# MLP and GLU up products: one 512-column matmul for high weights against both operand parts, and the two sums added by ScalarE and VectorE

## The reference, cut to what matters

```python
def _sq_relu_mlp(x, w1, w2):                 # w1: 1024 x 4096, w2: 4096 x 1024, twice
    return jnp.square(jax.nn.relu(x @ w1)) @ w2

def swiglu(h, w_gate, w_up, w_down):         # 1024 x 2816 twice, 2816 x 1024; twice
    return (jax.nn.silu(h @ w_gate) * (h @ w_up)) @ w_down
```

## Time and profile before

| what | value |
|---|---|
| median of 3 runs | 1182.96 us (1181.51 to 1185.43) |
| profiled execution, first to last instruction (span) | 1181.9 us |
| PE busy | 1162.1 us, 98% of the span |
| PEld, DVE, ACT, POOL busy | 1041.8, 658.0, 514.1, 51.0 us |
| share of PE in the chain that ended last | 92% |
| mean DMA rate | 169 GB/s |
| mean granted TensorE clock | 0.993 of full |

### The profile page before, as it was taken

One profiled execution on the slowest core, in us unless ns is written; L12 is line 12 of the kernel. 1 busy time (PEld: TensorE's weight loads), 2 busy tenths in 40 slices (PEclk: granted clock), 3 DMA queues, 4 the chain that ended last, 5 costly groups with the idle time before them and its releaser, 6 DMA issues.

```text
span 1181.9 us, 18506 instructions
## 1 busy us (share of the span) xinstructions
PE 1162.1 (98%) x7660; PEld 1041.8 (88%) x7668; DVE 658.0 (56%) x717; ACT 514.1 (43%) x581; POOL 51.0 (4%) x93
## 2 busy tenths in 40 slices
PE   9999999999999999999999999999999999999997
PEld 7997999998977799999889999989988878999996
DVE  4757554555654755545654544467854565544543
ACT  4433444443544344444344443445635644434342
POOL 1000000000200100000000000010120010000000
PEclk9999999999999999999999999998989999999999
DMA  9664656554641565565346555556651144456541
GB/s 338 220 211 146 213 178 197 182 180 120 211 161 36 177 219 179 190 183 187 127 144 213 178 177 177 198 156 202 192 164 37 37 161 139 149 181 206 189 148 54
DMA packets 140908, 199.67 MB, mean 169 GB/s; under 512 B 9240, under 2 KB 119024, under 8 KB 140864
## 3 DMA queue, kind: packets, MB, share of 16 engines
q1 hardware_dynamic: 138160, 190.27, 50.0%
q0 software_dynamic: 2704, 8.79, 2.4%
HBM read 197.99 MB, written 1.05 MB: 168 GB/s over the span
## 4 chain that ended last, share of the span: by engine, by line
PE 92%; DVE 3%; ACT 2%; DMA 2%; POOL 1%; issue 1%; SPq 0%; DVEq 0%; POOLq 0%; ACTq 0%
PE up L1401 15%; PE up L1403 15%; PE up L1402 15%; PE acc L1434 11%; PE acc L1435 11%; PE acc L1437 11%; DMA raw<-in_sc_w_in 2%; PE acc L1507 1%; PE up L1489 1%; PE up L1850 1%; PE up L1876 1%; PE up L1478 1%; PE up L1873 1%; PE up L1743 1%; PE up L1423 1%; PE up L1427 1%
## 5 line engine op out<-in xcount | busy, mean ns | idle before, releaser
L933 DVE TENSOR_TENSOR weight_lo<-raw,weight_hi 128x2048 fp32r<-128x2048 f32 (+3 forms) x206 | 414.4, 2017 | 312.4 <-ACT weight_hi L569 312.2
L1401 PE MATMUL up<-xh,weight_hi 128*128 128x256 f32 x1548 | 441.3, 285 | 1.9 <-ACT cols L569 0.8
L569 ACT ACTIVATE weight_hi<-raw 128x2048 fp32r<-128x2048 f32 (+3 forms) x206 | 347.3, 1693 | 213.6 <-PE acc L1437 119.7
L1402 PE MATMUL up<-xl,weight_hi 128*128 128x256 f32 x1548 | 438.9, 283 | 0.0
L1403 PE MATMUL up<-xh,weight_lo 128*128 128x256 f32 x1548 | 438.8, 283 | 0.0
L1401 PEld LDWEIGHTS up<-xh,weight_hi 128*128 128x128 f32 x1548 | 297.8, 192 | 5.9 <-issue 1.7
L1402 PEld LDWEIGHTS up<-xl,weight_hi 128*128 128x128 f32 x1548 | 297.9, 192 | 2.7 <-issue 0.7
L1403 PEld LDWEIGHTS up<-xh,weight_lo 128*128 128x128 f32 x1548 | 297.7, 192 | 0.0
L1434 PE MATMUL acc<-weight_hi,hh 128*128 128x512 f32 x480 | 187.6, 391 | 0.6 <-DVE hl L933 0.4
L1435 PE MATMUL acc<-weight_lo,hh 128*128 128x512 f32 x480 | 187.5, 391 | 0.0
L1437 PE MATMUL acc<-weight_hi,hl 128*128 128x512 f32 x480 | 150.3, 389 | 0.0
(11 more groups left out here) (215 smaller groups left out, 892.7 us busy)
## 6 DMA issues: line engine op xcount, KB each, us to landing
raw<-in_ff_w SPq DMA_DIRECT2D x64, 1024.0 KB, 5.7
raw<-in_ffn_w_gate SPq DMA_DIRECT2D x22, 1024.0 KB, 5.3
raw<-in_ffn_w_up SPq DMA_DIRECT2D x22, 1024.0 KB, 5.4
raw<-in_ffn_w_down SPq DMA_DIRECT2D x44, 512.0 KB, 4.7
raw<-in_w_in SPq DMA_DIRECT2D x16, 1024.0 KB, 5.7
raw<-in_sc_w_in SPq DMA_DIRECT2D x11, 1024.0 KB, 7.3
raw<-in_w_out SPq DMA_DIRECT2D x6, 1024.0 KB, 5.0
raw<-in_sc_w_out SPq DMA_DIRECT2D x4, 1024.0 KB, 5.3
```

What stands on the lines that cost most here:

```text
L569: return nc.scalar.activation(dst, src, ACT.Copy, **kw)
L933: return vec.tensor_tensor(dst, whole, high.bitcast(F32), ALU.subtract)
L1401: mm(dst, w_h, xh[:, x_tile + k, :], start=first and k == 0, stop=False)
L1402: mm(dst, w_h, xl[:, x_tile + k, :], start=False, stop=False)
```

## The change

The high and low parts of the operand lie side by side in one tensor `x_parts`, so that for one k they are 512 neighbouring columns, and the four banks `up` are one tensor. For each block f and each k, `wide_product` issues one matmul of 512 columns (high weights by high and low operand, into the two halves of a whole bank) and one of 256 columns (low weights by high operand, into the first half): 32 matmuls for a slab, which now takes two banks. In the first slab of a part, block f = 0 keeps three matmuls of 256 columns for each k, with the low operand's last. The two half banks are added outside TensorE: ScalarE copies the small half, VectorE adds it to the main half. In the GLU the gate product is always in banks 0 and 1 and the up product in banks 2 and 3, and TensorE waits for `summed` of the chunk before. The short convolution, MLA and hybrid products keep `up_product`.

```diff
-        xh = sb("xh", [P, KD, TOKENS], F32R)
-        xl = sb("xl", [P, KD, TOKENS], F32R)
+        x_parts = sb("x_parts", [P, KD, 2, TOKENS], F32R)
+        xh, xl = x_parts[:, :, 0, :], x_parts[:, :, 1, :]
...
+        def main_part(b):
+            return up_banks[:, b:b + CT, 0:TOKENS]
+        def small_part(b):
+            return up_banks[:, b:b + CT, TOKENS:HALF]
...
@@ ScalarE, mlp_part @@
-                    nc.scalar.activation(tmp_a[:, :], up[par][:, :], ACT.Relu).then_inc(q["relu"], 1)
+                    copy(pair(tmp_a[:, :]), small_part(2 * par)).then_inc(q["small_out"], 1)
...
-                            act.wait_ge(q["chunk"], 2 * it + (1 + j // 2))
-                            relu(0, par)
+                            act.wait_ge(q["summed"], 2 * it + (1 + j // 2))
+                            small_out(par)
...
@@ ScalarE, glu_part @@
+                def small_out(dst, b):
+                    copy(pair(dst[:, :]), small_part(b)).then_inc(q["small_out"], 1)
+                def gate():
+                    nc.scalar.activation(tmp_c[:, :], tmp_a[:, :], ACT.Silu).then_inc(q["gate"], 1)
...
                         if j % 4 == 0:
                             act.wait_ge(slab_used, off + (n + 1))
-                            act.wait_ge(q["chunk"], chunk + (1 + j // 4))
-                            gate(par)
+                            act.wait_ge(q["hidden"], chunk + (1 + j // 4))
+                            small_out(tmp_a, 0)
+                        if j % 4 == 1:
+                            act.wait_ge(q["summed"], 2 * chunk + (3 + 2 * (j // 4)))
+                            gate()
+                            act.wait_ge(slab_used, off + (n + 1))
+                            small_out(tmp_b, 2)
                         rounded(n + RING)
...
@@ VectorE, mlp_part (hidden_lo now stands before split_slab) @@
-                    vec.tensor_tensor(tmp_b[:, :], tmp_a[:, :], tmp_a[:, :], ALU.mult).then_inc(q["squared"], 1)
+                    vec.tensor_tensor(pair(tmp_b[:, :]), main_part(2 * par), pair(tmp_a[:, :]), ALU.add)\
+                        .then_inc(q["summed"], 1)
+                    dve.wait_ge(q["summed"], c)
+                    vec.scalar_tensor_tensor(tmp_c[:, :], tmp_b[:, :], 0.0, tmp_b[:, :], ALU.max, ALU.mult)\
+                        .then_inc(q["squared"], 1)
...
@@ VectorE, glu_part @@
-                    vec.tensor_tensor(tmp_b[:, :], up[2 * par + 1][:, :], tmp_a[:, :], ALU.mult)\
-                        .then_inc(q["hidden"], 1)
+                def summed(n, b, t):
+                    dve.wait_ge(q["small_out"], n)
+                    vec.tensor_tensor(pair(t[:, :]), main_part(b), pair(t[:, :]), ALU.add).then_inc(q["summed"], 1)
+                def gated(c):
+                    dve.wait_ge(q["gate"], c)
+                    dve.wait_ge(q["summed"], 2 * c)
+                    vec.tensor_tensor(tmp_d[:, :], tmp_b[:, :], tmp_c[:, :], ALU.mult).then_inc(q["hidden"], 1)
...
@@ TensorE @@
+            def wide_product(m, b, fresh=None):
+                for f in range(CT):
+                    bank = up[b + f]
+                    main, small = bank[:, 0:TOKENS], bank[:, TOKENS:HALF]
+                    w_h, w_l = [[w[:, m % RING, k * CHUNK_F + f * P:k * CHUNK_F + f * P + P] for k in range(KD)]
+                                for w in (weight_hi, weight_lo)]
+                    late = fresh is not None and f == 0
+                    for k in range(KD):
+                        if late:
...
+                            mm(main, w_h[k], xh[:, k, :], start=k == 0, stop=False, skip_group_check=True)
+                        else:
+                            mm(bank.rearrange("p (a n) -> p a n", a=2), w_h[k], x_parts[:, k, :, :], start=k == 0,
+                               stop=k == KD - 1, skip_group_check=True)
+                        ins = mm(main, w_l[k], xh[:, k, :], start=False, stop=k == KD - 1, skip_group_check=True)
+                    if late:
+                        pe.wait_ge(operand_low, 4 * fresh + 4)
+                        for k in range(KD):
+                            ins = mm(small, w_h[k], xl[:, k, :], start=False, stop=k == KD - 1, skip_group_check=True)
+                ins.then_inc(slab_used, 1)
...
@@ TensorE, glu_part @@
                         if j % 4 < 2:
-                            up_product(m, up[2 * par + j % 4])
+                            pe.wait_ge(q["summed"], 4 * it + (1 + j % 4 + 2 * (j // 4)))
+                            wide_product(m, 2 * (j % 4))
```

More of the change, by code:

```diff
@@ L177, in two_blocks @@
         acc = ctx.enter_context(nc.psum_tensor("acc", [P, 4, HALF], F32))
-        up = [ctx.enter_context(nc.psum_tensor(f"up{i}", [P, HALF], F32)) for i in range(4)]
+        up_banks = ctx.enter_context(nc.psum_tensor("up", [P, 4, HALF], F32))
+        up = [up_banks[:, i, :] for i in range(4)]
         ident = cst[:, C_ID:C_ID + P]
@@ L263, in two_blocks @@
         sc = Sems("sc", "c_copied ch_made conv0 y_made y_hi chunk")
-        mlp = [Sems(f"mlp{i}", "relu squared hidden_hi chunk") for i in range(2)]
-        glu = [Sems(f"glu{i}", "gate hidden hidden_hi chunk") for i in range(2)]
+        mlp = [Sems(f"mlp{i}", "small_out summed squared hidden_hi chunk") for i in range(2)]
+        glu = [Sems(f"glu{i}", "small_out summed gate hidden hidden_hi chunk") for i in range(2)]
         mla = Sems("mla", "rows latent_ps sumsq rstd latent turned t_hi t_lo pe q_out swapped rotated k_ps k_out v0 v1")
@@ L681, in mlp_part @@
                 act.wait_ge(slab_used, n + 1)
-                act.wait_ge(q["chunk"], FF_CHUNKS - 1)
-                relu(0, 1)
+                act.wait_ge(q["summed"], FF_CHUNKS - 1)
+                small_out(1)
                 act.wait_ge(q["squared"], FF_CHUNKS)
@@ L689, in glu_part @@
                 s, q = S_SG[i], glu[i]
-                def gate(par):
-                    nc.scalar.activation(tmp_a[:, :], up[2 * par][:, :], ACT.Silu).then_inc(q["gate"], 1)
+                def small_out(dst, b):
+                    copy(pair(dst[:, :]), small_part(b)).then_inc(q["small_out"], 1)
+                def gate():
+                    nc.scalar.activation(tmp_c[:, :], tmp_a[:, :], ACT.Silu).then_inc(q["gate"], 1)
                 def hidden_hi(par):
-                    copy(hh[:, CT * par:CT * par + CT, :], tmp_b[:, :].rearrange("p (f n) -> p f n", f=CT))\
-                        .then_inc(q["hidden_hi"], 1)
+                    copy(hh[:, CT * par:CT * par + CT, :], pair(tmp_d[:, :])).then_inc(q["hidden_hi"], 1)
                 act.wait_ge(slab_used, s + 1)
-                gate(0)
+                small_out(tmp_a, 0)
                 round_slab(s + RING)
+                act.wait_ge(q["summed"], 1)
+                gate()
+                act.wait_ge(slab_used, s + 2)
+                small_out(tmp_b, 2)
                 round_slab(s + 1 + RING)
@@ L1064, in _, with hidden_lo, squared @@
             followers(S_FF[0] - 1)
-            def hidden_lo(par):
-                return rest(hl[:, CT * par:CT * par + CT, :], tmp_b[:, :].rearrange("p (f n) -> p f n", f=CT),
-                            hh[:, CT * par:CT * par + CT, :])
+            def hidden_lo(par, whole):
+                return rest(hl[:, CT * par:CT * par + CT, :], pair(whole[:, :]), hh[:, CT * par:CT * par + CT, :])
             def mlp_part(i):
                 s, q = S_FF[i], mlp[i]
-                def square():
-                    vec.tensor_tensor(tmp_b[:, :], tmp_a[:, :], tmp_a[:, :], ALU.mult).then_inc(q["squared"], 1)
-                dve.wait_ge(q["relu"], 1)
-                square()
+                def squared(c, par):
+                    vec.tensor_tensor(pair(tmp_b[:, :]), main_part(2 * par), pair(tmp_a[:, :]), ALU.add)\
[3 more added lines that the diff above has]
+                        .then_inc(q["squared"], 1)
+                dve.wait_ge(q["small_out"], 1)
+                squared(1, 0)
+                dve.wait_ge(q["hidden_hi"], 1)
+                hidden_lo(0, tmp_c).then_inc(q["chunk"], 1)
                 split_slab(s + RING)
-                dve.wait_ge(q["hidden_hi"], 1)
-                hidden_lo(0).then_inc(q["chunk"], 1)
                 with dve.Fori(0, FF_CHUNKS // 2 - 1) as it:
@@ L1085, in mlp_part @@
                         if j % 2 == 0:
-                            dve.wait_ge(q["relu"], 2 * it + (2 + j // 2))
-                            square()
+                            dve.wait_ge(q["small_out"], 2 * it + (2 + j // 2))
+                            squared(2 * it + (2 + j // 2), par)
+                            dve.wait_ge(q["hidden_hi"], 2 * it + (2 + j // 2))
+                            hidden_lo(par, tmp_c).then_inc(q["chunk"], 1)
                         split_slab_at(n + RING, 4 * it)
-                        if j % 2 == 0:
-                            dve.wait_ge(q["hidden_hi"], 2 * it + (2 + j // 2))
-                            hidden_lo(par).then_inc(q["chunk"], 1)
                 n = s + N_FF - 3
```

(28 more changed lines are left out.)

24 lines of the change are left out of this document (16 added, 8 removed).

## The result

| | median of runs, us | lowest to highest | against the kernel before |
|---|---|---|---|
| before | 1183.51 (4 runs) | 1181.51 to 1185.43 | |
| changed kernel | 1176.64 (4 runs) | 1174.60 to 1178.61 | ratio 0.9942, 95% interval 0.9924 to 0.9960 |

The change gains 6.9 us, 0.6% (by the interval 4.7 to 9.0). The forecast was 1169.7 (1165.5 to 1175.0), a gain of 13.3: right in sign, nearly twice too large, and the measured time lies outside its range.

A forecast was written before the change was run, and what follows sets the result against it. The prediction took the kernel as bound by TensorE's one queue of matmuls; -14.8 us from joined up-product matmuls plus 1.5 us at the MLP ends gave -13.3, so 1182.96 becomes 1169.7 us, range about 1165.5 to 1175.

The forecast's parts named there:

- the gain of the up products: Up slabs: two 256-column matmuls (0.2400 us) become one of 512 (0.2275), saving 0.0125 on 1184 pairs, 14.8 us.
- The bounds of the prediction: Wide matmul's pitch: from 0.216 us (gain 28.4 us) to 0.240 us (no gain).
- the MLP ends: End of each MLP: add, release and longer square lengthen the exposed chain by 0.77 us, 1.5 us for both.
- The counts: 76 up slabs, 1216 pairs, less 4 x 8 in the four first slabs: 1184 joined pairs.
- no new wait of TensorE for the adds: MLP and GLU loops: VectorE's sums are ready well before TensorE needs them, so nothing is late.
- the moved `hidden_lo`: MLP loop: VectorE waits for it before `split_slab`, ending the split some 1.4 us later; costed at nothing.
- the GLU ends: End of each GLU: copy and add put 1.3 us ahead of `gated`, `hl` still 1.3 us early; costed at nothing.
- the table load: GLU's start: Silu's 1.28 us load falls between first copy and `gate`, while TensorE runs the first up slab; nothing late.
- the weight stream: Weights must stream at 174 (MLP) and 189 GB/s (GLU), with DMA busy share under 0.6; costed at nothing.
- VectorE late in the GLU: Rival, chance 0.03: TensorE waits for `summed` before gate or up products; at 2 us a chunk the time is 1209.7.
- The fixed cost that stays: Rival, chance 0.06: the fixed cost does not go with the joined instruction; a pair saves 2.9 ns, time 1181.1.
- The clock: Rival, chance 0.28: one half-clock stretch in the hybrid part, about 3.2 us, goes or is added: 1166.5 or 1172.9.

The follow-up runs named there:

- the grouped kernels: Changed kernel with the wide matmuls put first, then the narrow ones, within each block (1171.41 us) or within each slab (1170.05 us).
- grouping by slab: Changed kernel with all 16 wide matmuls of a slab first, then its 16 narrow ones; 1170.05 us, ratio 0.9872 to the kernel before.
- four and four: Changed kernel with four wide, then four narrow matmuls in turn; MLP chunk 11.071 us.
- two and two: Changed kernel with two wide, then two narrow matmuls in turn; MLP chunk 11.013 us, 1171.25 us, ratio 0.9891 to the kernel before.
- grouped by block: Changed kernel with each block's eight 512-column matmuls first, then its eight 256-column ones; 1171.41 us, ratio 0.9891 to the kernel before.

## Why the prediction was wrong

**The step that failed** is the gain of the up products: "I take 0.2275, because the down product has the same type, the same width and a fresh weight load for each matmul." That distance holds between like matmuls: in the down product, in the grouped kernels and in the kernel with 512 columns throughout (226.7 ns). It doesn't hold where every matmul is followed by one of another width. There a pair takes 353 ns (0.120 of it for the narrow one leaves 0.233 for the wide), the saving is 6 to 7 ns a pair and not 12.5, and on 1184 pairs that is some 7.5 us and not 14.8. The bounds of the prediction, 0.216 to 0.240, held it, but the range was cut as if the middle were known. The hint was in the timeline of before, in the same down product as the earlier trace rows, right behind the narrow matmuls:

```profile
204.85 0.40 PE L1434 MATMUL acc<-weight_hi,hh 128*128 128x512 f32 x1
...
205.55 0.40 PE L1435 MATMUL acc<-weight_lo,hh 128*128 128x512 f32 x1
```

Those are three distances, 0.233 each; 206.24 to 206.69 is two of 0.225 to 0.227. I took the mean over all 24 and so lost the difference.

**The sum redone.** An MLP chunk falls from 11.220 to 11.107 us, 0.113 for its one up slab; 30 whole slabs give 3.4 us. A GLU chunk falls from 16.98 to 16.79 us, only 0.187 for its two: in its down product nine of the first ten matmuls stand above 0.227, where before it was the first five. The 20 later chunks give 3.7 us. The first chunks of the four parts, with half of a slab left as it was, add some 0.4. Of these 7.5 us, 2 x 0.72 at the MLP ends go off again, which leaves 6.1. The medians have 6.9, and 6.1 is inside their interval.

**What held.** The counts (1184 pairs); no new wait of TensorE for the adds, in no loop; the moved `hidden_lo`, the GLU ends, the table load and the weight stream at nothing (chunks of 11.220 and 16.980 us with all of it in, and only the joined matmul out); the MLP ends at 0.72 us each, forecast 0.77 (the square took 692 ns and not 748).

**The rivals.** VectorE late in the GLU: no such wait, 9.5 us busy in 16.79. The fixed cost that stays: wrong as put, since an instruction among its like does carry its 13 ns away (grouping by slab takes the kernel from 1185.85 to 1170.05: 15.8 us, 15.2 by the ratio, where the forecast's pitch had 13.3), but it named the right place, and a mixture of it with the forecast would have been nearer. The clock: the profiled execution has no stretch at 0.50 in 860 to 885 us, and one is left, at 799 to 805 us; of its span's 9.3 us of difference some 3 are that (one stretch fewer, 3.2 by the prediction's estimate). The 6.1 us that remain of the span are the sum above.

**Open.** What inside TensorE makes the price, and why runs of two narrow matmuls cost 3.3 ns with 256 columns and 27 ns with 384. Shown is that it needs two widths, and that a new bank, at either step, doesn't take it away, nor is it the operands or the alternation of high and low weights.

## What to carry to other kernels

Where TensorE is the bound, joining matmuls saves the fixed cost of each one joined, but take the distance of a matmul from a row in which its neighbours are the ones that it will have. Put matmuls of one width together and measure the order: here the same instructions in another order gave some 6 us, nearly as much as the whole change. Longer runs were not better at every step (four and four lost to two and two), and with 384 columns no run longer than two was tried. And when a bound lies between two measured rows, keep it in the range, even if one of them looks like the same operation.

## What the runs showed of the hardware

Start to start, with a fresh weight load each, fp32r matmuls among their like take 120.0 ns for 256 columns and 226.7 for 512, so columns / 2.4 GHz + 13.3 ns. The Trainium skill, "TensorE: Matmul & The Clock Gate", section "Back-to-back issue gap", has 2.5 ns in that place, for a matmul by itself, and says that in a stream of weight loads and matmuls the distance is another. The fp32r matmuls with weight loads disagree with its 2.5 ns (13.3 in the grouped kernels), and the matmuls on zeros (0.216 us for 512 columns) agree. Behind eight or more narrow ones five matmuls of 512 columns take 228 to 236 ns before they are back at 227, and the first narrow one behind a run of wide ones takes 113 (traces of the kernels grouped by block and by slab); the two together are the 20 ns of a run. At the half clock 16 and 256 columns both stand 213 ns apart, which for 256 columns is columns / 1.2 GHz, so there the fixed cost doesn't show.
